# Attention loops in another order, one-pass row copies in the scan, row-half updates and a re-ordered norm in a two-block transformer kernel

## Time and profile before

| | us |
|---|---|
| median of 3 runs | 2097.2 (2095.29 to 2099.6) |
| the profiled execution | 2100.07 |
| its span in the trace | 2098.4 |
| TensorE busy | 2035.6 |
| VectorE busy | 1144.8 |
| ScalarE busy | 791.9 |
| mean granted TensorE clock | 0.986 of full |

### The profile page before, as it was taken

One profiled execution on the slowest core, in us unless ns is written; L12 is line 12 of the kernel. 1 busy time (PEld: TensorE's weight loads), 2 busy tenths in 40 slices (PEclk: granted clock), 3 DMA queues, 4 the chain that ended last, 5 costly groups with the idle time before them and its releaser, 6 DMA issues.

```text
span 2098.4 us, 23983 instructions
## 1 busy us (share of the span) xinstructions
PE 2035.6 (97%) x9845; PEld 1674.2 (80%) x9845; DVE 1144.8 (55%) x1692; ACT 791.9 (38%) x1117; POOL 90.3 (4%) x102
## 2 busy tenths in 40 slices
PE   7999999999999999999999899999999999999995
PEld 6887688878888888888888587888888888888884
DVE  5757547477544676366368777743435443234245
ACT  5547443244422434133242535542233333133142
POOL 0004300110000000000000300000000000000000
PEclk9999899999999999999999999999999999999998
DMA  4320022211323233332333123222322232322231
GB/s 130 101 81 22 1 93 88 81 61 61 132 90 101 81 101 101 101 88 83 111 121 101 41 72 99 80 81 101 101 92 89 82 99 101 101 92 89 101 118 53
DMA packets 164442, 184.46 MB, mean 88 GB/s; under 512 B 6759, under 2 KB 125798, under 8 KB 164334
## 3 DMA queue, kind: packets, MB, share of 16 engines
q1 hardware_dynamic: 160718, 173.98, 25.9%
q10 hardware_dynamic: 2912, 6.83, 1.0%
q0 software_dynamic: 704, 2.13, 0.3%
HBM read 180.81 MB, written 2.12 MB: 87 GB/s over the span
## 4 chain that ended last, share of the span: by engine, by line
PE 92%; DVE 4%; ACT 3%; issue 1%; DMA 0%; POOL 0%; DVEq 0%; ACTq 0%
PE ps L435 28%; PE ps L437 28%; PE ps L436 28%; PE ps L576 1%; PE ps L590 1%; ACT arena L1302 1%; PE ps L563 1%; PE ps L780 1%; PE ps L807 1%; PE ps L624 1%; DVE X L2378 0%; DVE arena L1897 0%; PE ps L962 0%; ACT L1294 0%; ACT arena L1341 0%
## 5 line engine op out<-in xcount | busy, mean ns | idle before, releaser
L435 PE MATMUL ps<-HH,WH 128*128 128x512 f32 (+1 forms) x1464 | 563.2, 385 | 11.0 <-DVE HL L1908 9.7
L1791 DVE TENSOR_TENSOR WL<-W,WH 128x2048 fp32r<-128x2048 f32 (+2 forms) x162 | 366.2, 2261 | 365.1 <-ACT WH L1264 356.2
L437 PE MATMUL ps<-HH,WL 128*128 128x512 f32 (+1 forms) x1464 | 558.8, 382 | 0.0
L436 PE MATMUL ps<-HL,WH 128*128 128x512 f32 (+1 forms) x1464 | 558.8, 382 | 0.0
L1264 ACT ACTIVATE WH<-W 128x2048 fp32r<-128x2048 f32 (+2 forms) x163 | 307.3, 1887 | 294.4 <-DMA W<-in_w_ff_dram 116.6
L435 PEld LDWEIGHTS ps<-HH,WH 128*128 128x128 f32 x1464 | 277.8, 190 | 67.2 <-issue 10.1
L437 PEld LDWEIGHTS ps<-HH,WL 128*128 128x128 f32 x1464 | 277.7, 190 | 52.8
L436 PEld LDWEIGHTS ps<-HL,WH 128*128 128x128 f32 x1464 | 278.1, 190 | 51.4 <-issue 0.2
L435 PE MATMUL ps<-WH,arena_r 128*128 128x512 f32 (+1 forms) x616 | 239.7, 389 | 1.6 <-issue 1.6
L436 PE MATMUL ps<-WL,arena_r 128*128 128x512 f32 (+1 forms) x616 | 239.1, 388 | 0.0
L437 PE MATMUL ps<-WH,arena_r 128*128 128x512 f32 (+1 forms) x616 | 239.0, 388 | 0.0
(11 more groups left out here) (341 smaller groups left out, 2282.4 us busy)
## 6 DMA issues: line engine op xcount, KB each, us to landing
W<-in_w_in_dram SPq DMA_DIRECT2D x50, 1024.0 KB, 5.2
W<-in_w_ff_dram SPq DMA_DIRECT2D x32, 1024.0 KB, 5.2
W<-in_ffn_w_up_dram SPq DMA_DIRECT2D x44, 512.0 KB, 5.0
W<-in_w_gate_dram SPq DMA_DIRECT2D x16, 1024.0 KB, 5.1
W<-in_ffn_w_down_dram SPq DMA_DIRECT2D x10, 1024.0 KB, 5.0
W<-in_w_out_dram SPq DMA_DIRECT2D x8, 1024.0 KB, 5.0
W<-in_w_branch_dram SPq DMA_DIRECT2D x8, 1024.0 KB, 5.1
W<-in_w_br_ssm_dram SPq DMA_DIRECT2D x4, 1024.0 KB, 5.3
```

What stands on the lines that cost most here:

```text
L435: pe.matmul(out_, st[0], mv[0], start=first, stop=False)
L436: pe.matmul(out_, st[0], mv[1], start=False, stop=False)
L437: return pe.matmul(out_, st[1], mv[0], start=False, stop=last)
L1791: dve.tensor_tensor(WL[:, j % RING, 0:n], W[:, j % RING, 0:n], plain(WH[:, j % RING, 0:n]), ALU.subtract).then_inc(slab_lo, 1)
```

## The change

- In both attention loops the `outputs` of odd steps are issued before the `turns`.
- VectorE's four slab parts come one step later in each loop (25 to 28, and 9 to 12); ScalarE's stay.
- The row copies of the scan become one fp32r product each over 48 rows: VectorE writes the high part of the rows of SS and, at rows 32 to 47, the rest, into the memory of `mask`, and a matrix `pick` with two ones in each column. GpSimd waits for the last use before it writes `mask` again.
- `updates` uses the 64 rows that aren't zero, and alternates between the two halves of the rows and two banks.
- The root of the norms takes in the scale and epsilon on ScalarE (bias from hb[:, 6:7]); VectorE no longer makes the variance there. A root of one element is done ahead of the norm, so that the function table is loaded then. In the norms after the first, VectorE scales tile t - 1 after adding tile t, and does the low parts of the first half in two lots of four, before the scaled tiles 2 and 3.
- At the start, only the first gain is loaded before slab 0 and turned alone (bank "gain"); the other eight parameter loads come after slab 0 on SP's queue, and their transpose between the halves of the first product. Slab 1 is split before the second half's evictions.

New semaphores norm_root, one_in and gain_in carry these. The diff, cut to its core:

```diff
@@ -120,6 +123,7 @@
         drow = sb("drow", [P, SH])
+        pick = sb("pick", [P, SH], F32R)
@@ -508,11 +516,13 @@
-            def gemm_f_by_halves(name, w, tiles):
+            def gemm_f_by_halves(name, w, tiles, between=None):
...
                     if half == 1:
+                        if between is not None:
+                            between()
@@ -596,11 +606,11 @@
                     scores(step)
-                    if step >= LAG:
-                        turns(step - LAG)
...
                         outputs(step - LAG - 1)
+                    if step >= LAG:
+                        turns(step - LAG)
@@ -632,14 +642,18 @@
                 pe.wait_ge(consts, 1)
-                pe.wait_ge(first_params_in, 16 * len(first_params))
-                pe.transpose(bank(("par", 0))[:, 0:P], rows[:, 0, :], ident[:, :]).then_inc(pe_done, 1)
+                pe.wait_ge(gain_in, 16)
+                pe.transpose(bank("gain")[:, 0:KT], rows[0:KT, 0, :], ident[0:KT, 0:KT]).then_inc(pe_done, 1)
             def pe_mla():
...
+                def first_parameters():
+                    pe.wait_ge(first_params_in, 16 * (len(first_params) - 1))
+                    pe.transpose(bank(("par", 0))[:, 0:P], rows[:, 0, :], ident[:, :]).then_inc(pe_done, 1)
...
                     if i == 0:
-                        gemm_f_by_halves("c", w, 2)
+                        gemm_f_by_halves("c", w, 2, first_parameters)
@@ -777,8 +792,8 @@
                             h = 4 * q + j
-                            mm = pe.matmul(b[:, j * P:(j + 1) * P], bc(ident[0:SH, h:h + 1], [SH, P]),
-                                           SS[0:SH, tok], start=True, stop=True)
+                            mm = pe.matmul(b[:, j * P:(j + 1) * P], bc(pick[0:48, h:h + 1], [48, P]),
+                                           decay_pieces[:, tok], start=True, stop=True)
@@ -956,13 +971,16 @@
                     taken(pe, ("gv", NT - 1, 0))
-                    for c in range(c0, c0 + 4):
-                        b = bank(("upd", c))
+                    for c in range(c0, c0 + 4, 2):
+                        two = [bank(("upd", c)), bank(("upd", c + 1))]
                         for pair in range(2):
-                            mm = pe.matmul(b[:, pair * 256:(pair + 1) * 256],
-                                           kz[:, c // 2, c % 2, pair * P:(pair + 1) * P],
-                                           v[:, c // 2, pair * 256:(pair + 1) * 256], start=True, stop=True)
-                        mm.then_inc(pe_done, 1)
+                            for j in range(2):
+                                rs = slice(64 * j, 64 * j + 64)
+                                mm = pe.matmul(two[j][:, pair * 256:(pair + 1) * 256],
+                                               kz[rs, c // 2, j, pair * P:(pair + 1) * P],
+                                               v[rs, c // 2, pair * 256:(pair + 1) * 256], start=True, stop=True)
+                                if pair == 1:
+                                    mm.then_inc(pe_done, 1)
@@ -1119,10 +1137,13 @@
             sp.wait_ge(rows_zero, 1)
-            for ap, start, n in first_params:
-                sp.dma_start(rows[start % P:start % P + n, start // P, 0:ap.shape[1]], ap)\
-                    .then_inc(first_params_in, 16)
+            ap, start, n = first_params[0]
+            sp.dma_start(rows[start:start + n, 0, 0:ap.shape[1]], ap).then_inc(gain_in, 16)
             for i, (kt, cols, pieces) in enumerate(slabs):
+                if i == 1:
+                    for ap, start, n in first_params[1:]:
+                        sp.dma_start(rows[start % P:start % P + n, start // P, 0:ap.shape[1]], ap)\
+                            .then_inc(first_params_in, 16)
@@ -1171,6 +1192,7 @@
             def pool_init():
+                pool.memset(hb[:, 7:8], 1.0).then_inc(one_in, 1)
@@ -1180,6 +1202,7 @@
                 chunk_mask()
+                pool.memset(hb[:, 6:7], EPS)
@@ -1233,6 +1256,7 @@
             def pool_convin():
+                taken(pool, ("ai", NT - 1, 3))
@@ -1298,10 +1322,12 @@
-            def square(t):
+            def square(t, nth):
...
                     .then_inc(ssq_ready, 1)
-                root(stat[:, t:t + 1])
+                act.wait_ge(ssq_ready, SSQ[nth] + t + 1)
+                act.activation(stat[:, t:t + 1], stat[:, t:t + 1], ACT.Sqrt, bias=hb[:, 6:7], scale=1.0 / DM)\
+                    .then_inc(norm_root, 1)
@@ -1312,21 +1338,26 @@
                 if tag is None:
+                    act.wait_ge(one_in, 1)
+                    act.activation(hb[:, 7:8], hb[:, 7:8], ACT.Sqrt)
...
                         act.wait_ge(x_in[t], 16)
-                        square(t)
+                        act.wait_ge(consts, 1)
+                        square(t, n)
...
                         split_piece(0, q)
-                    taken(act, ("par", 0))
+                    taken(act, "gain")
                     evict(0)
+                    split(1)
...
                 act_only_splits(tag)
+                act.activation(hb[:, 7:8], ones[:, 0:1], ACT.Sqrt)
...
                     taken(act, (tag, t, 1))
-                    square(t)
+                    square(t, n)
@@ -1754,7 +1786,7 @@
                     act.wait_ge(ple_added, 2 * t + 2)
-                    square(t)
+                    square(t, "final")
@@ -1892,15 +1924,15 @@
-                dve.wait_ge(ssq_ready, SSQ[nth] + t + 1)
-                rstd(stat[:, t:t + 1], DM)
+                dve.wait_ge(norm_root, NT * NORMS[nth] + t + 1)
+                link(dve.reciprocal(stat[:, t:t + 1], stat[:, t:t + 1]))
...
-                def lows(half):
+                def lows(half, k0=0, k1=KT):
                     cols = slice(half * S // 2, (half + 1) * S // 2)
-                    for k in range(KT):
+                    for k in range(k0, k1):
@@ -1920,12 +1952,15 @@
                         made(t)
-                    b = use(dve, ("par", 0))
-                    freed(dve.tensor_copy(par[:, 0:P], b[:, 0:P]), ("par", 0))
-                    taken(dve, ("par", 0))
+                    b = use(dve, "gain")
+                    freed(dve.tensor_copy(par[:, 0:KT], b[:, 0:KT]), "gain")
+                    taken(dve, "gain")
...
                     lows(0)
+                    split(1)
+                    b = use(dve, ("par", 0))
+                    freed(dve.tensor_copy(par[:, KT:P], b[:, KT:P]), ("par", 0))
@@ -1934,9 +1969,12 @@
                     add(tag, t, 1)
-                    if t == NT - 1:
-                        lows(0)
-                    made(t)
+                    if 1 <= t < NT - 1:
+                        made(t - 1)
+                lows(0, 0, KT // 2)
+                made(NT - 2)
+                lows(0, KT // 2, KT)
+                made(NT - 1)
@@ -2103,8 +2141,8 @@
                         split_piece(slab_of["z", 0, 0] - 1, step % 4, True)
-                    if 24 <= step < 28:
-                        split_piece(slab_of["z", 0, 0], step % 4)
+                    if 25 <= step < 29:
+                        split_piece(slab_of["z", 0, 0], (step - 1) % 4)
@@ -2152,6 +2190,11 @@
                 ins.then_inc(ssm_rows, 1)
+                dve.wait_ge(ssm_rows, 1)
+                decay_pieces = mask_r[0:48, :]
+                dve.tensor_tensor(pick[0:48, :], ident[0:48, 0:SH], ident[0:48, 32:32 + SH], ALU.add)
+                link(dve.tensor_copy(decay_pieces, SS[0:48, :]))
+                dve.tensor_tensor(decay_pieces[32:48, :], SS[0:SH, :], plain(decay_pieces[0:SH, :]), ALU.subtract)
@@ -2420,8 +2463,8 @@
                 def beside_scores(step):
-                    if 8 <= step < 12:
-                        split_piece(slab_of["sv", 0, 0], step % 4)
+                    if 9 <= step < 13:
+                        split_piece(slab_of["sv", 0, 0], (step - 1) % 4)
```

More of the change, by code:

```diff
@@ L106, in build @@
         ones = sb("ones", [P, P])
+        with ExitStack() as again:
+            mask_r = again.enter_context(nc.sbuf_tensor("mask_r", [P, S], F32R))
         mask = sb("mask", [P, S])
@@ L215, in build @@
         norm_low = sem("norm_low")
+        norm_root = sem("norm_root")
+        one_in = sem("one_in")
+        gain_in = sem("gain_in")
         mask_ready = sem("mask_ready")
@@ L393, in loaded @@
             return sum(len(slabs[j][2]) for j in range(i % RING, i + 1, RING))
+        NORMS = {0: 0, 1: 1, 2: 2, 3: 3, 4: 4, "final": 5}
         SSQ = {0: 0, "ssm": 4, 1: 8, 2: 12, 3: 16, 4: 20, "final": 24}
@@ L1363, in act_mla @@
                 cg, sq = split_at(2048, 5, S), at(15360, 5, S)
+                taken(act, ("par", 0))
                 for i in range(5):
```

## The result

The changed kernel takes 2079.5 us (median; 2076.5 to 2081.4), the kernel before 2098.4 in the same comparison: a ratio of 0.991, 95% interval 0.9891 to 0.9929. It is faster, by 19 us where 33 were summed up, and its time lies outside the predicted range of 2052 to 2077.

The account below looks back on a forecast made before the run. TensorE, busy for 97% of the span, was taken as the bound. Terms 9.7 + 2.6 + 4.2 + 5.3 + 9.9 + 0.9 + 0.6 = 33.2 us gave a forecast median of 2064 us, range 2052 to 2077.

Parts of the forecast that it names:

- Outputs ahead of the turnings: Odd steps of both attention loops: turnings no longer cover the bank-copy wait, 0.8 us more each; 5.6 and 2.4 us lost.
- the tail of the heads' loop at 10 to 11 us for four steps and a clock of 1.00: Predicted sign at the heads' loop's end: with slab parts a step later, quiet steps at full clock, against 19.69 us before.
- rival (c): Both attention loops stay disturbed, TensorE's clock falls at their ends anyway; 10.4 us lost back, time 2074; chance 0.13.
- The two loops' terms: Net gains in the attention loops, slab parts less reordering: heads 4.2 us, band 5.3 us.
- the parts' term: VectorE's slab parts a step later in both attention loops: 9.8 us gained in the heads' loop, 7.7 in the band's.
- Row copies: Scan: 16 groups of four copies, each 0.47 us instead of 1.08, save 9.7 us.
- The 0.118: Scan: time in us taken for one short fp32r row copy, from L807's 16 records in 1.89 us.
- Norms: Norms two to five: VectorE's new order cuts TensorE's waits for low parts and the clock falls after; 9.9 us gained.
- Updates: Gated updates: 64-row products in alternating array halves save 2.6 us over eight groups, the middle of 1.8 and 3.4.
- the 0.4 to 0.6: Predicted sign in the gated updates: us per group of two products, against 0.85 before.
- Start and end: Kernel's first product 0.9 us earlier (between 0 and 2.8); last tiles' chains without a hop, 0.6 us gained.
- From the sum to the median: Whole kernel: 2066.9 us for the profiled execution, less 2.9 for its lying above the runs' median, gives 2064.

## Why the prediction was wrong

**Outputs ahead of the turnings: mechanism right, place and size nearly right, its consequence missed.** Ten stops before first outputs are there, eight of them for the copy of the bank; the first of each loop waits for turned weights instead. Seven in the heads' loop sum to 7.9 us and three in the band's to 4.3, against 1.7 and 1.5 with the turnings first (the 1.5 counts 0.6 for a turning that then waits for GpSimd): 9.0 us lost where eight were summed up. A quiet stop loses 0.65 (0.86 against 0.21) where 0.8 was taken; three stops have a part of VectorE just ahead of the copy, 0.5 to 0.6 each, which the prediction left in the range. One of these is a part in step 23, of the slab before: VectorE splits parts in steps 20 to 23 too, which the text on the kernel before doesn't name.

**The step that failed** is "the tail of the heads' loop at 10 to 11 us for four steps and a clock of 1.00": the sum of both loops took quiet steps at full clock and put the fall of the clock into rival (c). The clock fell in both, behind waits of 1.58 and 1.69 us, and took 5.1 us; with the 9.0 that makes the 13.9 of the table, within 0.2, and half of rival (c)'s 10.4 came. The two loops' terms were 9.5 together and 3.4 were measured: of the 6.1 that are missing, the clock is 5.1. With the turnings first it held at both ends, in the four kernels that have the parts a step later. The size of the parts' term was right: 10.2 and 7.2 measured alone, against 9.8 and 7.7.

That the longer wait brings the clock down is likely, but not that it does so each time. In the heads' loop the clock fell in five of the six traces with the waits of 1.58, and in none of the six with the parts a step later and no wait over 1.3 us. In the band's loop it fell in all six traces with the wait of 1.69, in five of them at that wait or right behind it, but it fell near the loop's start too, in one kernel even with the turnings first. And in the kernel with the old norm order the heads' loop has the same waits, and its last steps ran at full clock:

```profile
233.39:244.26 10.87, 9.03 (x73) 6.20 (x73) 8.19 (x31) 6.68 (x20) 5.18 (x5) 1.00 0.01 3
```

Its loop took 87.4, 3.4 less than 90.7. What decides between two such executions is open.

**Row copies: a term of the sum mis-sized.** 9.7 summed up, 6.6 measured. The 0.118 for one product was right (0.112); the group has 0.14 of its own, which makes 0.59 instead of 0.47 and 16 x 0.12 = 1.9 us. The other 1.2 are the two waits for slabs: TensorE came earlier than VectorE's low part, a thing that is late next and that the prediction didn't look for. L780's groups may contain the same price (8 x 0.118 + 0.14 is their 1.08, an estimate), so the earlier trace rows couldn't tell it apart; the distance from a group to a group of other size would have. The 0.118 itself was the duration of L807's row over 16, with its pipeline; by the distance to the next row, 409.45 - 407.62, it is 0.114.

**Norms: near in size, with one of two sufficient causes.** 9.9 summed up, 8.6 measured. The prediction named VectorE's order, and the new order alone does bring the wait down to 0.37; but the order wasn't needed, since the early table load alone brings it to 0.63, and that load was in the trace at 677.04. The 0.36 that stays stands behind ScalarE's first eviction, which waits 0.96 us for TensorE to turn a bank, and VectorE's low part 0.69 for it; the prediction had 0 to 0.1. The clock held in all norms: 7.95 us for what took 9.46 in the third.

**Updates:** 2.9 against 2.6: 16 records now take 1.92 us to the next product, 0.48 a group, inside the 0.4 to 0.6. The first call took 3.26 before, not 3.4.

```profile
1325.84 2.00 PE L979 MATMUL ps<-arena 64*128 64x256 f32 x16
1327.76 1.42 PE L1013 MATMUL ps<-arena 128*64 128x128 f32 x22
```

**Start and end.** One execution can't tell. The first product came 0.67 us earlier, at 15.35 against 16.02; then its successors came at the lower level's pace from the first on, where the kernel before did nine at full pace:

```profile
15.70 0.41 PE L444 MATMUL ps<-HL,WH 128*128 128x256 f32 x1
15.91 0.41 PE L445 MATMUL ps<-HH,WL 128*128 128x256 f32 x1
```

0.21 apart, against 0.12. (The granted clock reads 1.00 there all the same; the distances are what tells.) Over all traces the heads' loop began at 158.8, 159.7 and 160.6 with the old start (mean 159.7) and between 156.9 and 159.8 with the new (eleven, mean 158.9): 0.8 less, against 0.9 summed up, in a scatter of 2 to 3 us, so that a gain there isn't shown. At the end the hop brought 0.1 instead of 0.2 for the last tile, and from the end of VectorE's last 1024-wide addition to the end of the span it took 3.8 us against 3.0.

**From the sum to the median.** The prediction subtracted 2.9 us, since its execution lay so far above the median of three runs. Later medians of the same kernel were 2097.6, 2100.2 and 2098.1, and 2098.4 beside the changed kernel: the execution lay 1.7 above that, and the rest of the 2.9 was scatter. The changed kernel's own execution lay 1.2 below its median. So by the two executions 11.4 us of the miss of 15.5 are in the sum, and 4.1 in this step.

**Luck, 1.5 us of it:** in the profiled execution of the kernel before the clock fell at 1269.61, in that of the changed one not:

```profile
1269.61:1273.35 3.74, 3.74 (x10) 2.93 (x10) 3.74 (x6) 3.58 (x4) 0.63 (x1) 0.54 0.52 183
```
```profile
1255.40:1257.61 2.21, 2.21 (x11) 1.80 (x11) 2.21 (x4) 2.05 (x3) 0.63 (x1) 1.00 0.89 312
```

The first is the kernel before, the second the changed one, over the same nine products and the start of the next: 1.5 us. No edit touches them, and the fall is no property of either kernel: from the band's loop to the first update it was 119.8 to 119.95 us in six of the 14 traces, four of them of kernels with the whole change in this place, and 118.3 to 118.4 in the other eight.

## What to carry to other kernels

Work that TensorE has at hand belongs ahead of the operand that comes late: moving it behind turned a covered wait of about 1 us into a bare one, ten times, and in the traces that show it the falls of the clock added half as much again. When one of two copies that release a product is moved forward, the other is the next bound, so list all releasers of a wait before you move one. And where a chain runs from tile to tile through two engines, look for the table load in it too; taking the load out and taking the chain apart are two cures for one wait, and their gains don't add. Last, compare two single traces stretch by stretch only beside a third: 1.5 us in one stretch and 3.4 in another came and went between executions of the same instructions.

## What the runs showed of the hardware

- A group of short one-pass products between large ones has a price of its own, 0.14 us here by groups of four and eight, beside 0.112 for each product with a load of 128 columns.
- The clock falls in single stretches that cost 1.5 to 6.9 us each (6.9 at the end of the heads' loop before), at places that recur (the first products, the ends of the loops, the first products of a norm, products in the gates of block two), but in one execution and not in another of the same code there: the heads' last steps with the same waits ran at 0.69 in five traces and at 1.00 in one. A comparison of two single traces has this as its scatter.
- Two 64-row products in the two halves of the array, in a row of four groups, cost 0.48 us for 256 columns each, against 0.63 for one such pair alone among other work and 0.82 to 0.89 for two products over 128 rows before.
